# Product-key experts: those with a low second key computed densely from two streamed tables

## What is computed

```python
q = (xb @ w_q).reshape(n, 8, 2, 128)                     # 8 heads, two half keys
s = einsum('thpk,pnk->thpn', q, sub_keys)                # 128 scores on each side
s_top, i_top = top_k(s, 16)
cand_s = s_top[:, :, 0, :, None] + s_top[:, :, 1, None, :]
cand_i = i_top[:, :, 0, :, None] * 128 + i_top[:, :, 1, None, :]
best_s, best_pos = top_k(cand_s, 16)                     # 16 of 256 pairs
idx = cand_i[best_pos]                                   # of 16,384 experts
gate = softmax(best_s)
act = gelu(einsum('thkd,td->thk', down[idx], xb))        # rows of 1024 floats
out = einsum('thk,thkd->td', gate * act, up[idx])
```

## Time and profile before

| | |
|---|---|
| time, median of 3 runs | 2350.69 us (2349.46 to 2351.3) |
| the profiled execution | 2351.76 us, its span 2350.0 us |
| granted PE clock, mean | 0.891 |
| PE / DVE / ACT / POOL busy | 77% / 49% / 27% / 25% |
| DMA, mean over the span | 366 GB/s |
| gathers of layer 0, layer 1 issued | 211.9 to 862.1, 919.9 to 1562.0 us |

### The profile page before, as it was taken

The page is one execution under the profiler, slowest core; times in us unless marked ns, Lnnn a source line. Parts: engine busy times, 40 slices in busy tenths (PEclk is TensorE's granted clock), DMA queues, the critical chain, the costliest instruction groups (busy, mean ns, idle before and its releaser), DMA issues.

```text
span 2350.0 us, 25585 instructions
## 1 busy us (share of the span) xinstructions
PE 1799.8 (77%) x9657; PEld 768.5 (33%) x9657; DVE 1162.3 (49%) x2865; ACT 645.8 (27%) x1813; POOL 589.4 (25%) x516
## 2 busy tenths in 40 slices
PE   7999776656555567776555555569989999999998
PEld 3455442111111125442111111114445544444443
DVE  2335766676767556766676767554534311111111
ACT  2242333332333322333332333332432210000001
POOL 0001444444444431354444444430000000000000
PEclk9999998677778889997887778779999999999999
DMA  9596999999999987999999999996313399999996
GB/s 392 224 425 266 408 420 420 419 420 418 417 407 420 410 345 316 412 420 420 420 420 420 416 417 421 416 387 256 117 57 144 152 410 427 427 428 426 428 427 263
DMA packets 98217, 861.19 MB, mean 366 GB/s; under 512 B 11406, under 2 KB 11534, under 8 KB 12844
## 3 DMA queue, kind: packets, MB, share of 16 engines
q0 software_dynamic: 73728, 536.90, 55.3%
q1 hardware_dynamic: 24364, 322.62, 33.0%
HBM read 858.44 MB, written 1.05 MB: 366 GB/s over the span
## 4 chain that ended last, share of the span: by engine, by line
PE 45%; DMA 36%; DVE 8%; ACT 5%; issue 3%; POOL 3%; SPq 0%; POOLq 0%; DVEq 0%; ACTq 0%
DMA arena<-in_experts,arena 28%; PE bank L2021 12%; PE bank L2711 9%; PE bank L2359 8%; DMA ring<-in_experts,arena 5%; PE bank L2757 5%; DVE arena L1484 3%; PE bank L2721 2%; POOL arena L701 2%; PE bank L2125 2%; ACT arena L908 2%; PE bank L2137 1%; DMA arena<-in_w_up 1%; PE bank L2654 1%; ACT arena L903 1%
## 5 line engine op out<-in xcount | busy, mean ns | idle before, releaser
L2359 PE MATMUL bank<-arena 64*64 64x512 f32 x2080 | 342.5, 788 | 258.7 <-ACT arena L908 258.5
L2359 PE MATMUL bank<-ring,arena 64*64 64x512 f32 x2016 | 335.8, 796 | 227.9 <-ACT arena L908 227.6
L701 POOL DMA_INDIRECT arena<-in_experts,arena x260 | 300.3, 1155 | 655.9 <-PE bank L2359 347.2
L1484 DVE SCALAR_TENSOR_TENSOR arena<-arena,h 128x1024 f32<-128x1024 f32 x260 | 320.3, 1232 | 225.6 <-DMA arena<-in_experts,arena 224.0
L1484 DVE SCALAR_TENSOR_TENSOR ring<-ring,h 128x1024 f32<-128x1024 f32 x252 | 310.0, 1230 | 210.1 <-DMA ring<-in_experts,arena 209.4
L701 POOL DMA_INDIRECT ring<-in_experts,arena x252 | 288.9, 1146 | 318.3 <-PE bank L2359 275.7
L899 ACT ACTIVATE arena<-arena 128x2 f32<-128x2 f32 x256 | 52.1, 203 | 851.8 <-DVE arena L1484 466.5
L2359 PEld LDWEIGHTS bank<-arena 64*64 64x64 f32 x2080 | 80.9, 161 | 485.9 <-ACT arena L908 373.2
L2359 PEld LDWEIGHTS bank<-ring,arena 64*64 64x64 f32 x2016 | 79.6, 164 | 465.2 <-ACT arena L908 359.7
L2711 PE MATMUL bank<-ring,arena 128*64 128x512 f32 x768 | 223.5, 593 | 1.7 <-ACT arena L1101 1.2
L908 ACT ACTIVATE arena<-const,arena 128x128 f32<-128x128 f32 x512 | 177.6, 394 | 8.4
(11 more groups left out here) (430 smaller groups left out, 1829.6 us busy)
## 6 DMA issues: line engine op xcount, KB each, us to landing
ring<-in_w_gate SPq DMA_DIRECT2D x32, 2048.0 KB, 14.8
ring<-in_mod_w SPq DMA_DIRECT2D x20, 2048.0 KB, 11.5
arena<-in_w_up SPq DMA_DIRECT2D x16, 2048.0 KB, 20.9
arena<-in_w_down SPq DMA_DIRECT2D x16, 2048.0 KB, 15.9
ring<-in_w_up SPq DMA_DIRECT2D x16, 2048.0 KB, 16.3
ring<-in_w_down SPq DMA_DIRECT2D x16, 2048.0 KB, 11.5
ring<-in_w_in SPq DMA_DIRECT2D x9, 2048.0 KB, 7.3
ring<-in_peer_w_q SPq DMA_DIRECT2D x8, 2048.0 KB, 12.9
```

The lines of the kernel that those rows point to most:

```text
L701: pool.indirect_dma_start(out=gslot(l, n), out_offset=None, in_=a["experts"], in_offset=bass.IndirectOffsetOnAxis(ap=idx_all[:, t, at:at + ...
L1484: ins = v.scalar_tensor_tensor(out=row, in0=row, scalar=1.0, in1=h[:, t], op0=ALU.mult, op1=ALU.mult, accum_out=act[:, t, HEAD * hh + k:HE ...
L2359: ins = pe.matmul(bank[2 * t + r][out_rows, :], diag[own_rows, PER * (j % 2) + k, own_rows], row[own_rows, 512 * c:512 * c + 512], start=j ...
```

## The change

Experts with j < 16 (`DENSE`; 2048 of 16,384) are no longer gathered. For every one of them and every token the kernel computes gelu of the product with its `down` row, multiplies by a gate that is zero where the token did not pick the expert, and sums the `up` rows.

- Host arrays `dense_down` and `dense_up`: per layer eight pieces each of 128 rows of 8 KB, in the order of use. SP streams the 16 pieces of a layer (`load_tables`) into one ring place, two halves in turn, each when PE has used the piece before the last.
- `top_k`'s last step adds 32,768 to the index of a pick with j < 16; the gathers carry `bounds_check=32767, oob_is_err=False`. Number, size and order of the gathers stay. `gates` keeps the whole gate in `picks` and sets that of such a pick in `gate` to zero.
- The selection steps now run one behind every gather, a set in 16 gathers, so that all picks are known by gather 128.
- PE computes the field (2048 experts by 256 tokens) in 32 parts of four products of 256 columns, j = 31 to 62 (`product_part`); ACT takes gelu of it (`field_out`). `turn_picks` turns the picks of each tile to have tokens along the row. For each group of eight tokens DVE builds one-hots of i and of j times gate (`one_hots`, gathers 134 to 196, every second), PE multiplies them (`spread_gates`, eight products of 16 columns, j = 67 to 98), DVE multiplies the field by the result (`weigh`). Then 32 parts of four quarter products with the `up` pieces (`sum_part`, j = 103 to 122), tile 0 in banks 4 and 5 and added by `add_dense` behind gather 249, tile 1 into its running sums in banks 2 and 3.
- Since tile 0 is complete only then, its norms and turns, and `pool_bands(0)`, move behind the gathers. pool_w's successors: the third peer_w_q load of layer 1 and the second w_in load wait for `x_peer` (the second `add_experts` of the layer), because their ring place holds its scratch.

The core of the diff:

```diff
@@ SP
+            def load_tables(l):
+                for p in range(2 * PIECES):
+                    if p < 2:
+                        sem, value = piece_free(l)
+                        sp.wait_ge(S[sem], value)
+                    else:
+                        sp.wait_ge(S["piece_used"], counted("piece_used", 2 * PIECES * l + p - 1))
+                    table = a["dense_down"] if p < PIECES else a["dense_up"]
+                    sp.dma_start(piece(l, p), table[l, p % PIECES]).then_inc(S[f"piece_landed{p % 2}"], 16)
...
             load_weights("wq0_last", 1)
+            load_tables(0)
             sp.wait_ge(S["up_used"], GROUPS)
...
             load_weights("wq1_last", 1)
+            load_tables(1)
             wait_gathered(sp, 1, PICKS * NT - 1)
@@ POOL
-                        in_offset=bass.IndirectOffsetOnAxis(ap=idx_all[:, t, at:at + 1], axis=0)).then_inc(
+                        in_offset=bass.IndirectOffsetOnAxis(ap=idx_all[:, t, at:at + 1], axis=0),
+                        bounds_check=2 * EXPERTS - 1, oob_is_err=False).then_inc(
@@ DVE, top_k and gates
+                        link(v.tensor_scalar(sel[:, 1, cut], picks[:, 1, t, here], DENSE - 0.5, float(FAR), ALU.is_lt, ALU.mult))
+                        link(v.tensor_tensor(sel[:, 0, cut], sel[:, 0, cut], sel[:, 1, cut], ALU.add))
...
+                    v.scalar_tensor_tensor(out=g3, in0=keys_j, scalar=DENSE - 0.5, in1=whole, op0=ALU.is_gt,
+                                           op1=ALU.mult).then_inc(S["gates"], 1)
@@ DVE, one_hots and weigh
+                    link(v.tensor_tensor(hot_j(l, g), bc(keys[:, 0:DENSE], 1, GROUP), bc(picked(l)[:, 1, at], 2, DENSE), ALU.is_equal))
+                    v.tensor_tensor(hot_i(l, g), bc(keys, 1, GROUP), bc(picked(l)[:, 0, at], 2, P), ALU.is_equal)
+                    v.tensor_tensor(hot_j(l, g), hot_j(l, g), bc(picked(l)[:, 2, at], 2, DENSE), ALU.mult).then_inc(S["hot_made"], 1)
...
+                    v.wait_ge(S["spread"], counted("spread", n + 1))
+                    part = field[:, :, GROUP * g:GROUP * g + GROUP]
+                    v.tensor_tensor(part, part, bank[SPREAD_BANK[n % 3]][:, 0:P].rearrange("p (u j) -> p j u", u=GROUP),
+                                    ALU.mult).then_inc(S["field_made"], 1)
@@ DVE, down(g)
-                        elif g < BLOCKS - 2 and n % 4 < 3 and n - n // 4 < STEPS:
-                            top_k(g // 2 + 1, n - n // 4)
+                            if g < 8 and k < STEPS:
+                                top_k(g, k)
+                        if n >= HOT_FROM and n % 2 == 0:
+                            if 0 <= (n - HOT_FROM) // 2 - 3 < TOKEN_GROUPS:
+                                weigh((n - HOT_FROM) // 2 - 3)
+                            if (n - HOT_FROM) // 2 < TOKEN_GROUPS:
+                                one_hots((n - HOT_FROM) // 2)
+                        if (g, k) == (BLOCKS - 1, 9):
+                            add_dense()
@@ PE
+                    for q in range(4 * (part % 2), 4 * (part % 2) + 4):
+                        ins = pe.matmul(bank[4 + p % 2][:, T * j:T * j + T], w[:, j, q], hT[:, q, :], start=q == 0, stop=q == KT - 1,
+                                        skip_group_check=True)
...
+                    for u in range(GROUP):
+                        ins = pe.matmul(bank[SPREAD_BANK[n % 3]][:, DENSE * u:DENSE * u + DENSE], hot_i(l, g)[:, u], hot_j(l, g)[:, u],
+                                        start=True, stop=True)
...
+                            ins = pe.matmul(bank[(4, 2)[t] + r][half_of(r ^ c), :], field[:, 2 * p + j, at:at + 64],
+                                            w[:, j, 512 * c:512 * c + 512], start=t == 0 and p == 0 and j == 0,
+                                            stop=t == 0 and p == PIECES - 1 and j == 1, skip_group_check=True)
@@ PE, behind the layers
             keep_warm(8, 0)
+            pe.wait_ge(S["in_const"], 32)
+            pool_bands(0)
             pool_bands(1)
...
+            pe.wait_ge(S["normed"], normed("nmix", 1))
+            tile_transposes(h, 0)
             pe.wait_ge(S["turned_ev"], turned("tmix", 2))
```

## The result

The kernel became slower: 2420.06 us, median of 4 runs (2411.66 to 2429.78), against 2350.99 us before (4 runs, 2349.46 to 2352.66). The ratio is 1.0292 (95% interval 1.0271 to 1.0313). The prediction was 2340, with a range up to 2366: the sign and the size were both wrong. The profiled execution has a span of 2416.4 us, 66.4 more than before.

A forecast was written before the change was run, and what follows sets the result against it. The prediction took the DMA engines, full with gathers, as the bound. Gathers and tables together -25, DVE +3, first key +1, behind layer 0 +2.4, behind layer 1 +8 summed to -10.6: 2340 us, range 2322 to 2366.

The forecast's parts named there:

- The bound: Both expert stages: the sixteen DMA engines are full (share 1.01) while PE, DVE and POOL are partly idle.
- The gathers lose rows: Gathers of both layers: skipped picks save 45 us in layer 0 and 60 in layer 1, by a gather-by-gather walk.
- The tables: Dense table loads among the gathers: 32 pieces at 2.5 us on the same engines, 40 us a layer.
- DVE: Selection steps, one-hots and weighing among the gathers: DVE about level with the transfers, +3 us, at most 18.
- PE: 0: Added products behind each pair of gathers: they sit in PE's gaps and slots come back no later, cost 0.
- First key: Ahead of each layer's first gather: two more linked instructions, +1 us for both layers, between 0 and 1.5.
- behind layer 0: After layer 0's gathers: tile 0's band products delay tile 1's, +2.4 us, bounds 1 and 5.
- behind layer 1: After layer 1's gathers: tile 0's norm and turns now come late, PE begins w_in later, +8 us, bounds 3 and 12.
- (a): Rival on the gathers: the bound spares no bytes or skipped rows still cost their time; 2445 us, chance 0.08.
- (c): Rival on the gathers: remaining rows are dealt evenly over the engines in the long run; 2296 us, chance 0.06.
- (b): Rival on the gathers: remaining rows are dealt anew, always from the first engine; 2364 us, chance 0.12.
- (d): Rival on the computing: DVE or PE becomes the bound, price +20 to +30, 2362 to 2372 us; chance 0.14.

The follow-up runs named there:

- s1: The changed kernel without its tables and without the whole dense computation: 2275.5 us, ratio 0.9685 to the kernel before.
- s2: The changed kernel without the dense computing alone; tables still loaded, one small product reads each piece: 2351.9 us, ratio 0.9999.
- s3: The changed kernel with one spreading product of 128 columns in place of eight of 16 (gates wrong): 2357.7 us, ratio 1.0032.
- s4: The changed kernel with the spreading products' operands exchanged, 16 columns loaded as weights and 128 streaming (dense experts wrong): 2357.2 us, ratio 1.0025.
- s7: The changed kernel with the one-hots and the gates in them in bfloat16, nothing left out: 2362.5 us, ratio 1.0038.
- s6: The changed kernel plus one product of constants, 512 columns wide, behind the narrow ones of 29 of 32 groups per layer: 2375.5 us, ratio 1.0113.
- t1: The changed kernel with spreading products on constants, so PE and DVE do not wait for each other's one-hots (gates wrong): 2384.8 us, ratio 1.0166.
- s8: The kernel before plus eight narrow fp32 products of constants (128 weight columns, 16 streaming) behind pairs 67 to 98 of both layers: 2368.5 us, ratio 1.0065.
- t2: The changed kernel with spreading products on constants and no one-hots written by DVE at all: 2386.5 us, ratio 1.0132.
- s9: The kernel before plus eight products of constants with 16 weight columns and 128 streaming behind pairs 67 to 98: 2352.2 us, ratio 1.0002.
- g_all_rows: The changed kernel with indices not moved past the bound, so picks with a low second key are gathered too: 2497.8 us, ratio 1.0603.

## Why the prediction was wrong, point by point

**The bound.** Right for the kernel before; in the changed one PE is the bound from about gather 128 to 224 of each layer.

**The gathers lose rows: -105.** Measured in s1: -93.6 (-44.1 and -49.5). The bytes and the packets were right. The gather-by-gather walk is 1 us off in layer 0 and 10 in layer 1. No run shows the 45 and 60 taken from the walk by themselves; in their place s1 showed 44.1 and 49.5. That a gather is served only with the last of its 16 landing updates the traces do show: in the kernel before they are spread over 3.9 us (median), and DVE's next product with h starts 24 ns (median) after the last. That each update is one engine's, and the last one that of the fullest, is the author's assumption; no row gives an engine's rows. Why layer 1 is short was not tested, and the deal by engine is only argued from these times.

**The tables: +80.** Measured between s2 and s1: +78.5. So these two terms gave -25 and were -15.

**DVE: +3.** The steps behind every gather did no visible harm: s1 contains them and meets the walk in layer 0. The one-hots and the weighing are in what s3, s4 and s7 lie above s2, 5 to 11 us for all the computing that is left; what of it is DVE's was not separated. Inside the bounds of 0 to 18.

**PE: 0.** This is the step that failed; it should have been some 60 (s3 and s4 lie 62 to 63 under the changed kernel, s7 58). The prediction priced the narrow products at 0.18 us an instruction, 2 to 3 us for eight, called the sum with the pair "under 5", and expected the clock to rise, because a window with 74.9 us of busy PE had been granted 0.91; so the new products were to sit in the gaps and the slots to come back no later. The instructions measured 1.96 us for eight at the upper clock, where the estimate was more than enough, and 3.59 at the lower. But the window it leaned on held query products, with 128 streaming columns, and it was the only evidence that busy time brings the clock. Of the products in the forecast the dense ones, with 256, behaved so (0.95 and 0.97 from 300 to 500), and the sums, with 512 (0.96 from 800 to 900, 0.93 from 1500 to 1600). PE at 96% with narrow ones stayed at 0.68. The missing question was not "how busy" but "what does this work look like beside the work that was granted the clock".

The clock did not follow PE's busy time as the profile has it: 95.9 of 100 us busy were granted 0.68 in the kernel after, 97.8 were granted 0.98 in s6, and in t1 PE is busy without a gap both from 688 to 703, at 1.00, and from 704.5 to 744, at 0.50. What the chip counts instead no row here tells.

**And then the coupling.** Even with the clock priced, a second piece was missing. Of the 68 us over s2, the waits between PE and DVE make some 35 (t1), and the products alone 16 in the kernel before (s8); the rest, under 20, is what other computing costs (s7 over s2: 10.5) and what these numbers are uncertain by. These are differences between different kernels, and that they add up is not shown. Two buffers of one-hots, made by an engine with 4.2 us of work a pair (from 670.88 to the next one-hots at 675.05 DVE has no gap), leave PE no pairs in reserve to run through while it has the upper clock.

**First key +1, behind layer 0 +2.4, behind layer 1 +8.** Measured +1.1, +2.5 and +9.1. The agreement to a tenth is partly luck: kernels with the same first stretch issue their first gather anywhere from 209.9 (t2) to 213.4 us (s7), the stretch behind layer 0 is 62.6 us in s1 and s2 against the 60.3 here, and s9, whose edit lies ahead of that stretch, takes 791.6 us behind the last gather and not 788.0. In the timeline behind layer 1, DVE takes the last gather at 1630.87 and PE begins with w_in at 1645.39, 14.5 us later, where 15 was predicted:

```profile
1630.87 1.23 DVE L1613 SCALAR_TENSOR_TENSOR arena<-arena,h 128x1024 f32<-128x1024 f32 x1 [0.94 <-DMA arena<-in_experts,arena]
...
1645.39 7.17 PE L2164 MATMUL bank<-ring,hT 128*128 128x512 f32 x12 [0.69 <-ACT hT L836]
```

**The rivals.** (a) is out: 470.0 MB, and s1 is faster. (c) is out: evenly dealt rows would have saved 71 and 88 us in s1. (b) expected +14 and -15 us with the tables in, the forecast -5 and -20; s2 has -3.4 and -11.7. Layer 0 speaks clearly against (b), layer 1 lies between the two and nearer to (b), so a fixed deal is the better account and not a proven one. (d) held the truth, with "PE at 1.2 GHz would need 3.7 + 3.7 us for a pair with products", close to the 3.69 + 3.59 measured. It got 0.14 and a price of 20 to 30, where it cost some 60: the price was taken from DVE's arithmetic and not from its own sentence. 64 pairs of 7.3 us against 5.0 would have been 147 us, an upper bound that the range should have leaned towards.

**The signs to look for.** "Gathers within 640 to 650 and 618 to 630" is what s2 did, but for half a microsecond (646.8 and 630.5), so the forecast describes the change without its computing. "Clock of PE above 0.85 in the products" held for the dense products and failed for the spreading (0.66 to 0.76). The mean clock of the whole span rose, from 0.891 to 0.915, while the kernel became slower: it says nothing of the stretch that binds. "DMA's share falls below 1 where there are no tables" was a bad sign to choose: it fell, for PE's sake, and in s1, where only unevenness was left, it read 1.00. In s1 the last column is lower, 401 GB/s from 600 to 700 against 410 before in the same stretch and 419 to 420 from 400 to 600; that fits unevenness.

## What to carry to other kernels

Price added PE work at both clocks (here 1.96 and 3.59 us), and take the lower one unless the added instructions themselves are like those that the profile shows at the upper; then ask whether the cheaper form (fewer products, another type, the operands exchanged) fits even at the lower clock. When a second engine feeds PE through two buffers, ask whether PE can still use a faster clock to catch up; here it could not, and two modest costs became one large one. Before a trade of transfers against computing is built, run it with the computing left out: here that kernel is a draw, so with this layout of tables and tails no computing, however good, could have won.

## What the runs showed of the hardware

- Adding 58 products of 512 columns to the changed kernel (s6) made it 44.6 us faster; exchanging the operands of the narrow ones (s4) raised the clock of the stretch from 0.68 to 0.97 at the same count of products.
- Eight products with 128 columns of weights and 16 streaming take 1.96 us in fp32 at the upper clock (1.00), 3.59 at the lower (0.50), and 0.36 us in bfloat16 (s7), where they are 8 matmul instructions in place of 16 and a weight load takes 96 ns in place of 192.
- A row past the bound is a packet of 4 bytes and some 9 ns (median of the 16,363 such packets after), so the packet count does not change (73728 before and after). Each gather's issue on POOL went from 0.937 to 0.992 us.
- The share of busy DMA engines can stay at 1.00 while less is moved (from 600 to 700, 410 GB/s before and 401 in s1). By the page a row of 8 KB took 317 ns of engine time before (55.3% of 16 x 2350.0 us for 65,536 rows) and 329 in s1 (51.9% of 16 x 2270.5 us for 57,353 rows). In the trace's packets the median hardly moves (313 and 311 ns), but the slowest in a hundred goes from 324 to 833 ns. With no row skipped but PE the bound (g_all_rows) it is 720, so the long packets fit engines that wait within a packet rather than dearer rows. That reading was not tested by itself.
